# Seven-product up chunks in the first plain feed-forward stage, and the weight sums of the gated stages on VectorE

## What is computed

```python
def _sq_relu_mlp(h, w_up, w_down):            # first block, twice: w_up 1024 x 4096
    u = jax.nn.relu(h @ w_up)
    return (u * u) @ w_down
...
x = x + _sq_relu_mlp(_rmsnorm(x, norm_ffn[i]), mlp_w_up[i], mlp_w_down[i])
...
# second block, four times: gate and up weights side by side, 1024 x (2 * 2816)
x = x + 0.5 * rms_norm(swiglu(rms_norm(x, g[0]), ffn_wgu[i, 0], ffn_wd[i, 0]), g[1])
```

## Time and profile before

| | |
|---|---|
| median of 3 runs | 3510.94 us (3510.49 to 3515.82) |
| the profiled execution | 3511.05 us |
| its span, first to last instruction | 3509.1 us |
| TensorE busy | 3423.1 us |
| VectorE busy | 2336.1 us |
| ScalarE busy | 1423.5 us |
| GpSimd busy | 940.0 us |
| mean granted TensorE clock | 0.991 of full |

### The profile page before, as it was taken

How to read it: one execution, slowest core, us unless ns; L and a number is a source line. 1 busy time by engine, 2 the same in 40 slices (tenths; PEclk the granted TensorE clock), 3 DMA queues, 4 the chain that set the end, 5 groups by cost and what they waited for, 6 DMA issues and landing times. The chain is left out here.

```text
span 3509.1 us, 54575 instructions
## 1 busy us (share of the span) xinstructions
PE 3423.1 (98%) x21451; PEld 2854.4 (81%) x21451; DVE 2336.1 (67%) x3142; ACT 1423.5 (41%) x2011; POOL 940.0 (27%) x627
## 2 busy tenths in 40 slices
PE   8999999999999999999999999999999999999998
PEld 6888888644789979997777789987998787778997
DVE  6665554366677778876567587878777534468786
ACT  5632223365444444334544343344334422244333
POOL 1220002010223325444014145424443000015452
PEclk9999999999999999999999999999999999999999
DMA  3332224100323223232200123222332222213322
GB/s 122 96 112 96 96 96 108 37 1 1 96 96 108 96 84 109 96 108 92 73 26 4 61 96 109 96 95 87 107 107 96 84 84 84 81 52 108 109 97 71
DMA packets 232575, 296.21 MB, mean 84 GB/s; under 512 B 21893, under 2 KB 201464, under 8 KB 232392
## 3 DMA queue, kind: packets, MB, share of 16 engines
q1 hardware_dynamic: 230864, 290.48, 25.6%
q0 software_dynamic: 1152, 3.05, 0.4%
q10 hardware_dynamic: 376, 0.12, 0.0%
HBM read 291.53 MB, written 2.10 MB: 84 GB/s over the span
## 5 line engine op out<-in xcount | busy, mean ns | idle before, releaser
L336 DVE TENSOR_TENSOR wlo<-raw,whi 128x2048 fp32r<-128x2048 f32 x266 | 654.0, 2458 | 265.2 <-ACT whi L330 252.8
L330 ACT ACTIVATE whi<-raw 128x2048 fp32r<-128x2048 f32 x191 | 365.6, 1914 | 691.6 <-PE bank L342 598.8
L340 PE MATMUL bank<-h_hi,whi 128*128 128x512 f32 (+1 forms) x1548 | 616.5, 398 | 23.6 <-DVE h_lo L1135 11.2
L341 PE MATMUL bank<-h_lo,whi 128*128 128x512 f32 (+1 forms) x1548 | 602.7, 389 | 0.0
L342 PE MATMUL bank<-h_hi,wlo 128*128 128x512 f32 (+1 forms) x1548 | 602.6, 389 | 0.0
L340 PE MATMUL bank<-u_hi,whi 128*128 128x512 f32 x1440 | 563.2, 391 | 10.9 <-DVE fsum L850 4.8
L342 PE MATMUL bank<-u_hi,wlo 128*128 128x512 f32 x1440 | 560.7, 389 | 0.0
L341 PE MATMUL bank<-u_lo,whi 128*128 128x512 f32 x1440 | 560.3, 389 | 0.0
L340 PEld LDWEIGHTS bank<-h_hi,whi 128*128 128x128 f32 x1548 | 292.1, 189 | 102.3 <-issue 27.2
L342 PEld LDWEIGHTS bank<-h_hi,wlo 128*128 128x128 f32 x1548 | 292.1, 189 | 61.0
L341 PEld LDWEIGHTS bank<-h_lo,whi 128*128 128x128 f32 x1548 | 292.3, 189 | 60.7 <-issue 3.6
(11 more groups left out here) (487 smaller groups left out, 5959.6 us busy)
## 6 DMA issues: line engine op xcount, KB each, us to landing
raw<-in_ffn_wgu SPq DMA_DIRECT2D x88, 1024.0 KB, 5.1
raw<-in_ffn_wd SPq DMA_DIRECT2D x44, 1024.0 KB, 4.8
raw<-in_mlp_w_up SPq DMA_DIRECT2D x32, 1024.0 KB, 5.3
raw<-in_mlp_w_down SPq DMA_DIRECT2D x32, 1024.0 KB, 4.8
raw<-in_odd_w_in SPq DMA_DIRECT2D x24, 1024.0 KB, 5.1
raw<-in_even_w_in SPq DMA_DIRECT2D x13, 1024.0 KB, 5.3
raw<-in_rg_w_in SPq DMA_DIRECT2D x8, 1024.0 KB, 5.6
raw<-in_odd_w_out SPq DMA_DIRECT2D x8, 1024.0 KB, 5.0
```

Source lines behind the costliest of these rows:

```text
L330: e.activation(whi[:, n % 2, :], raw[:, n % 2, :], ACT.Copy).then_inc(hi_ready, 1)
L336: e.tensor_tensor(wlo[:, n % 2, :], raw[:, n % 2, :], whi[:, n % 2, :].bitcast(F32), ALU.subtract).then_inc(lo_ready, 1)
L340: pe.matmul(o, w_hi, r_hi, start=first, stop=False)
L341: pe.matmul(o, w_hi, r_lo, start=False, stop=False)
```

## The change

f0 gets seven-product up chunks from group 4 on, and f1 from group 4 instead of 5. Both use the same token steps (two tiles before group 2, two before group 3), and both, as the gated stages do already, make the low halves of group 1 only behind the sixth eviction of the first down chunk. GpSimd's token sums wait for all eight token operations instead of four. The sparse mixer's constants, which lie where f0's token tiles now are, are made behind f0's last up chunk, except for the first clearing and the two transfers into `fsum`. The tables for even and odd are made behind the wait for VectorE's sums of the norm instead of ahead of it.

In the gated stages `dve_weights_sums` on VectorE takes the place of `pool_weights`. For the gate chunk of the next group it stands behind the fourth part of the up chunk (in the last plain group: at the end of the group); for the up chunk it stands at the very start of the group. The low copy of the up chunk moves from there to between the third and the fourth part of the gate chunk.

```diff
--- before.py
+++ after.py
@@ -121,7 +121,7 @@
         n_hi_a, n_lo_a = sem("n_hi_a"), sem("n_lo_a")
         w_hi, w_lo = sem("w_hi"), sem("w_lo")
         LEFT, RIGHT = slice(0, S // 2), slice(S // 2, S)
-        w_sum = sem("w_sum")
+        w_sum, v_sum = sem("w_sum"), sem("v_sum")
         xhi_ready, xlo_ready = sem("xhi_ready"), sem("xlo_ready")
         t_scaled, t_sum, t_hi, t_lo = sem("t_scaled"), sem("t_sum"), sem("t_hi"), sem("t_lo")
         seven_act, seven_dve = sem("seven_act"), sem("seven_dve")
@@ -192,7 +192,7 @@
             down = a["ffn_wd_2"][l, i].rearrange("(c k p) n -> c p k n", k=2, p=P)
             return dict(gu=2, groups=NG2, w=[g, u], down=down, swiglu=True, dst=fsum)
 
-        SEVEN = {"f1": 5, "s00": 3, "s01": 3, "s10": 3, "s11": 3}
+        SEVEN = {"f0": 4, "f1": 4, "s00": 3, "s01": 3, "s10": 3, "s11": 3}
 
         def seven(name, g):
 
@@ -456,11 +456,32 @@
             e.wait_ge(w_sum, at(4 * y + 3, i, 4 * k))
             e.tensor_tensor(d[:, XS4], quarter(n, 1, 0), d[:, XS2], ALU.subtract).then_inc(w_sum, 1)
 
+        def gated_no(name, g, c):
+            return seven_no(name, g, c) - seven_no("s00", SEVEN["s00"], 0)
+
+        def dve_weights_sums(e, name, g, c, n, i, dn):
+            y, z = seven_no(name, g, c), 4 * gated_no(name, g, c)
+            d = wsum[(y - seven_base[name]) % 2]
+            e.wait_ge(loaded[n % 2], at(landed[n], i, dn * 8))
+            if (y - seven_base[name]) % 2:
+                e.wait_ge(tiles_out, before[chunk_gu(name, SEVEN[name]) - 1])
+            e.wait_ge(xlo_ready, at(y - 1, i, 4))
+            e.tensor_tensor(d[:, XS3], quarter(n, 0, 0), quarter(n, 0, 1), ALU.subtract).then_inc(v_sum, 1)
+            e.wait_ge(v_sum, at(z + 1, i, 16))
+            e.tensor_tensor(quarter(n, 0, 1), quarter(n, 0, 1), quarter(n, 1, 1), ALU.add).then_inc(v_sum, 1)
+            e.wait_ge(v_sum, at(z + 2, i, 16))
+            e.tensor_tensor(d[:, XS2], quarter(n, 0, 1), quarter(n, 0, 0), ALU.subtract).then_inc(v_sum, 1)
+            e.wait_ge(v_sum, at(z + 3, i, 16))
+            e.tensor_tensor(d[:, XS4], quarter(n, 1, 0), d[:, XS2], ALU.subtract).then_inc(v_sum, 1)
+
         def act_weights(e, name, g, c, n, i, dn, dt, middle=None):
             k = 2 * FFN[name]["gu"]
             y = seven_no(name, g, c)
             e.wait_ge(tiles_out, at(before[n - 1], i, dt))
-            e.wait_ge(w_sum, at(4 * y + 4, i, 4 * k))
+            if FFN[name]["swiglu"]:
+                e.wait_ge(v_sum, at(4 * gated_no(name, g, c) + 4, i, 16))
+            else:
+                e.wait_ge(w_sum, at(4 * y + 4, i, 4 * k))
             e.activation(whi[:, n % 2, :], raw[:, n % 2, :], ACT.Copy).then_inc(hi_ready, 1)
             if middle:
                 middle()
@@ -527,7 +548,7 @@
             for h in range(2):
                 v = [th_raw[:, 2 * h:2 * h + 2, t, 0, :] for t in range(7)]
                 b12 = th_raw[:, 2 * h:2 * h + 2, TB11, 1, :]
-                e.wait_ge(t_scaled, 2 * z + h + 1)
+                e.wait_ge(t_scaled, 2 * z + 2)
                 e.tensor_tensor(v[T1], b12, v[TB11], ALU.subtract).then_inc(t_sum, 1)
                 e.tensor_tensor(v[T3], v[TB22], b12, ALU.subtract).then_inc(t_sum, 1)
                 e.wait_ge(t_sum, 8 * z + 4 * h + 1)
@@ -535,7 +556,7 @@
                 e.wait_ge(t_sum, 8 * z + 4 * h + 3)
                 e.tensor_tensor(v[T4], v[TB21], v[T2], ALU.subtract).then_inc(t_sum, 1)
 
-        TOKEN_STEPS = {"f1": {2: (0,), 3: (1, 2), 4: (3,)}}
+        TOKEN_STEPS = {name: {2: (0, 1), 3: (2, 3)} for name in ("f0", "f1")}
 
         def act_tokens(e, name, ks):
             z = t_no[name]
@@ -701,8 +722,8 @@
 
             def gu(g, n, i, dn, dt):
                 if seven(name, g):
-                    for c in range(f["gu"]):
-                        pool_weights(e, name, g, c, n + c, i, dn)
+                    if not f["swiglu"]:
+                        pool_weights(e, name, g, 0, n, i, dn)
                     return
                 if f["swiglu"]:
                     for j in range(2):
@@ -740,10 +761,11 @@
                         e.wait_ge(uhi_done, at(2 * (b + g - 1) + 2, i, 4))
                     src = part(c, P_E)
                     step(3 * c + 1)
-                    third = tmp[:, 7, LEFT] if meanwhile else d
+                    third = tmp[:, 7, LEFT] if c else d
                     e.tensor_tensor(third, src, snap[:, c, :], ALU.add).then_inc(seven_dve, 1)
                     if meanwhile:
                         meanwhile()
+                    if c and meanwhile:
                         e.wait_ge(ulo_done, at(2 * (b + g - 1) + 2, i, 4))
                     src = part(c, P_C)
                     step(3 * c + 2)
@@ -752,11 +774,14 @@
                 def outer(c, p, d, signal):
                     e.tensor_tensor(d, part(c, p), snap[:, c, :], ALU.add).then_inc(signal, 1)
                 if f["swiglu"]:
+                    dve_weights_sums(e, name, g, 1, n + 1, i, dn)
                     if deferred(name, g - 1):
                         products(g - 1, i)
+                joined(0)
+
+                def low():
                     dve_lo(e, n + 1, i, dn, dt)
-                joined(0)
-                last_quarter(0)
+                last_quarter(0, low if f["swiglu"] else None)
                 if f["swiglu"]:
                     dve_weights_rest(e, name, g, 1, n + 1, i)
                 elif deferred(name, g - 1):
@@ -770,6 +795,8 @@
                 dve_lo(e, n + 2, i, dn, dt)
                 joined(1)
                 last_quarter(1, (lambda: u_low(g - 1, i, (1,))) if deferred(name, g - 1) else None)
+                if seven(name, g + 1):
+                    dve_weights_sums(e, name, g + 1, 0, n + 3, i, dn)
                 src = part(1, P_A2)
                 e.wait_ge(seven_act, at(a0 + 2, i, 2 * acts))
                 e.tensor_tensor(tmp[:, 2, LEFT], src, tmp[:, 0, LEFT], ALU.mult)
@@ -823,8 +850,10 @@
                             e.wait_ge(ulo_done, at(2 * (b + g - 1) + j + 1, i, 4))
                         e.tensor_tensor(tmp[:, 2 + j, :], pbank[half + 2 + j][:, :], tmp[:, j, :], ALU.mult)\
                             .then_inc(prod_done, 1)
-                if not (g == 1 and f["swiglu"] and name in SEVEN):
+                if not (g == 1 and name in SEVEN):
                     u_low(g, i)
+                if f["swiglu"] and seven(name, g + 1):
+                    dve_weights_sums(e, name, g + 1, 0, n + 3, i, dn)
                 if g == 0 and not f["swiglu"]:
                     dve_lo(e, n + f["gu"] + 1, i, dn, dt)
                 if g == 0 and name in SEVEN:
@@ -855,7 +884,7 @@
                         e.tensor_tensor(dst[:, m, :], dst[:, m, :], src[:, :], ALU.add).then_inc(added, 1)
                     if final and early_lo(stage) and m >= 2:
                         lo_tile(e, stage + 1, m - 2)
-                    if m == 5 and g == 0 and f["swiglu"] and name in SEVEN:
+                    if m == 5 and g == 0 and name in SEVEN:
                         u_low(1, i)
                     if final and not early_lo(stage) and m == 1:
                         dve_lo(e, n + 1)
@@ -1032,11 +1061,11 @@
             j = norm_no[stage]
             if PLAN[stage][1] is not None:
                 pool_owed(e, stage)
+                e.wait_ge(n_add, 7 * j + 7)
                 if PLAN[stage + 1] == ("even",):
                     pool_even_early(e, chain)
                 elif PLAN[stage + 1] == ("odd",):
                     pool_odd_early(e, chain)
-                e.wait_ge(n_add, 7 * j + 7)
                 return
             if PLAN[stage - 1][0] == "setup":
                 for k in range(1, 4):
@@ -1737,14 +1766,20 @@
         def slope_of(h):
             return 2.0 ** (-8.0 * (h + 1) / HEADS)
 
+        def pool_nsa_first(e, chain):
+            chain(e.memset(fsum[:, :, :], 0.0))
+            for h in range(2):
+                r = slice(h * HD, h * HD + HD)
+                e.dma_start(w1bd[0][r, :, r], NSA_SMALL[0][0][0].rearrange("(l d) e -> d l e", d=HD)).then_inc(small_in, 16)
+
         def pool_nsa_early(e, chain):
-            chain(e.memset(fsum[:, :, :], 0.0))
+            last = FFN["f0"]["groups"] - 1
+            e.wait_ge(tiles_out, before[chunk_gu("f0", last) + 1])
+            e.wait_ge(gate_done, 2 * (ffn_base["f0"] + last) + 2)
             chain(e.memset(w2bd[:, :, :], 0.0))
             for z, (w1, w2, pe_) in enumerate(NSA_SMALL):
                 for h in range(2):
                     r = slice(h * HD, h * HD + HD)
-                    if z == 0:
-                        e.dma_start(w1bd[z][r, :, r], w1[0].rearrange("(l d) e -> d l e", d=HD)).then_inc(small_in, 16)
                     e.dma_start(w2bd[r, z, r], w2[0]).then_inc(small_in, 16)
                     e.dma_start(perow[0:CMP_LEN, z, r], pe_[0]).then_inc(small_in, 16)
             e.dma_start(gw[:, :, :], cols(nsa_in, D + 6 * 256, 48)).then_inc(small_in, 16)
@@ -3575,11 +3610,12 @@
```

(7 more changed lines are left out.)

## The result

The changed kernel takes 3531.48 us (median of 5 runs, 3529.13 to 3533.4) against 3511.58 for the one before (5 runs, 3510.49 to 3515.82): a ratio of 1.0055, 95% interval 1.004 to 1.007, so 19.9 us slower. The profiled execution took 3529.13 us with a span of 3527.4, which is 18.3 more than the 3509.1 of before. Two runs in a far slower state of the chip, one of the kernel before (4843 us) and one of e11 (6378 us), are left out of all ranges and ratios.

A forecast was written before the change was run, and what follows sets the result against it. TensorE, busy 98% of the span, was the bound. Terms -11.4 - 0.95 - 1.8 - 5.8 - 1.8 + 41.9 = +20.2 on 3511.05 gave 3531, put at 3530.5 us; range 3503 to 3550, its own 3520 to 3545.

The forecast's parts named there:

- f0 and f1, groups: Seven-product groups in f0 from group 4 save 11.4 us; f1 starting at group 4 instead of 5 saves 0.95.
- constants behind the last up chunk: Sparse mixer's constants moved behind f0's last up chunk: at most 19 us within a 21.8 us window, so zero cost.
- First down chunks: First down chunks lose their lateness: 1.8 us gained in f1, 5.8 over four gated stages, nothing lost in f0.
- Norms: Tables made after the norm's sums gain 1.5 us before even and 0.3 before odd; bounds 0 and 3 in all.
- The gated term: Gated stages: sums on VectorE delay TensorE's fifth and seventh products through a chain of order, costing 41.9 us.
- groups 4 to 9: Gated loop groups in four stages: 0.94 us of waits per group, 22.6 us in all.
- group 10: Unrolled gated group: slower sums and a join raise the wait to 1.35 us, 5.4 over four stages.
- Group 3: First seven-product gated pair: late sums make it near 22.7 us; with 0.6 lost ahead each time, 13.9 more.
- rival 1: Gated sums are hidden because VectorE is ahead at the down chunk's end: 3489 us, chance 0.16.
- Rival 2: Waits shorten TensorE's matmul pitch from 0.118 to some 0.113 us, giving back 13.8 us: 3517, chance 0.13.
- Rival 3: VectorE becomes the bound, each gated period longer by another 0.8 to 1.2 us: 3560, chance 0.08.
- Rival 4: Token and norm gains fail, GpSimd's scalings disturbing as before: +6, 3537 us; chance 0.63 together with the forecast.

The follow-up runs named there:

- e11: Version with both moves (e5), TensorE also waiting before each group's second product for the end of its own first product: 3512.08 us, ratio 1.0008.
- e9: Version with both moves (e5), group 1's low halves again ahead of the first down chunk's evictions in f0 and f1: 3495.94 us, ratio 0.9964.
- e6: Changed kernel with GpSimd's token sums again waiting for four token operations instead of eight: 3536.61 us, ratio 1.0076.
- e10: Version with both moves (e5), GpSimd's tables for even and odd again ahead of the wait for the norm's sums: 3494.56 us, ratio 0.9959.
- e5: Changed kernel, ScalarE's first-product copy ahead of its wait for the up chunk's sums, VectorE's low copy behind the fourth part: 3491.08 us, ratio 0.9947.
- e8: Changed kernel plus one useless 256-column VectorE addition per gated group, behind the gate chunk's sums: 3532.94 us, ratio 1.0064.
- run 118: Not a follow-up run: part of the sentence saying that matmuls of 256 columns run 118 ns apart; no kernel or measured time belongs to it.
- e3: Changed kernel with only ScalarE's copy of the gate chunk's first product moved ahead of its wait for the up chunk's sums: 3495.17 us, ratio 0.9959.
- e1: Changed kernel with gated sums back on GpSimd and the up chunk's low copy back ahead of the first join: 3492.75 us, ratio 0.9956.
- e2: Kernel before, with only the gated stages' sums moved to VectorE and the low copy's new place: 3557.83 us, ratio 1.013.

## Why the prediction was right

It gave 3530.5 us, 19.6 above before, with 3531.48 measured. Its steps, each against the changed kernel's trace:

- **f0 and f1, groups.** -11.4 and -0.95 predicted. From the sums of the norm ahead of f0 to those of the norm behind it took 360.0 us and takes 348.7, so -11.3; the same for f1, its first down chunk included, went down by 2.8, with -2.75 predicted. Groups at 20.81 as said; constants behind the last up chunk cost nothing that shows.
- **First down chunks.** f1 -1.8 and gated -5.8 predicted, -1.8 and -6.1 measured: f1 went from 12.64 to 10.88, and the gated stages from 12.33, 12.28, 12.66 and 12.31 to 10.88 each (the one that was read for the prediction stood for all). e9 and e6 give each back by its edit alone. f0 doesn't pay, as said. The reason given for the gated stages, half the operations still disturbed and a lead of 2 us left over, was too careful: two of these operations, which the changed kernel makes last, take 0.74, and evictions start (1296.98) 3.9 us behind the chunk, 1.5 ahead of need.
- **Norms.** -1.5 and -0.3 predicted, -1.45 and -0.23 measured, and 1.5 and 0.3 in e10.
- **The gated term.** +41.9 predicted. The pairs add up to 675.1 against 633.6, 41.5 more, and the four down chunks ahead of group 3 to 1.7 more: +43.2. The chain was named link by link: first sum 0.90 behind the start instead of 0.81, last one done at 3.76 (3.59), copy of the first product at 5.98 (5.81), fourth part at 9.52 (9.26). Two of its terms were a little small. The chained sums are 0.72 us apart, not 0.70, and the extra of a late release falls due at both waits, not once: 0.37 + 0.11 at the fifth product, 0.61 + 0.11 at the seventh, 1.19 per pair against 0.94. Against that stands the shorter pitch: six of the 32 pairs came out 0.41 to 0.43 us shorter than their like (five at 20.55 to 20.65, one of group 3 at 22.02), since behind the seventh product's wait their matmuls ran 0.113 apart. Group 3 was put at 22.7 and is 22.4, the wait ahead of it at 0.6 and is 0.43. So the parts were off by more than their sum: groups 4 to 9 cost 26.8 and not 22.6, group 10 4.9 and not 5.4, group 3 with the wait ahead of it 11.6 and not 13.9. That these errors nearly cancel is luck.
- **What the sum left out.** The steps as measured add up to +21.3 (-11.3 - 2.8 - 6.1 - 1.7 + 43.2), the span to +18.3. The missing 3.0: the start until f0 is 1.3 shorter, the stretch from s00 to s01 is 2.0 shorter beyond its norm's gain, of which 0.75 is a norm at half clock in the kernel before alone, and the sparse mixer is 0.3 longer. The mixer of even itself ran 10.2 us at half clock before and 6.8 after. Among the kept executions of the changed kernel and its variants, which share this code, the start spreads over 2.1 us, the stretch from s00 to s01 over 3.2 and the sparse mixer over more (last section). So a hit within 1 us is luck too; what the prediction can claim is the sign, the mechanism and the size of the main term.
- **Slips of the working.** Group 3's pairs and the waits ahead of them give 11.4 + 4 x 0.6 = 13.8, not 13.9; group 10's parts add up to 1.32, not 1.35; and with a third of the waits left rival 1 comes to 3503, not 3500. None moves the forecast.
- **The rivals.** Rival 1, sums hidden, said 3489 and falls as put: the chain does bind. But its number is e5's, 3491.08: the cover it asked for is there, and only the order keeps the kernel from it. Rival 2, the shorter pitch, was seen in 6 of 32 pairs; e11 shows that a wait by itself doesn't cause it. Rival 3, VectorE at its limit, falls by e8, by sums 0.72 us apart where it asked for 1.0, and by a period of 31.89 where it asked for over 32.3. Rival 4, disturbances that stay, falls by e6 and e10.
- **The rule.** By the Trainium skill (GPSIMD Engine Reference, section 4.1), VectorE is the place for such sums. The trace agrees for the single operation (0.69 against 1.29 us). For the kernel the rule gave no answer: 43 us lost with the sums in this order, none in the loop with e5's.

## What to carry to other kernels

A move of work to a faster engine is priced by what stands behind it in that engine's order, not by its load: here 5.6 us per group fitted under TensorE and still cost it 1.2, since two short operations that TensorE waited for stood behind long copies nobody needed yet. So when an input becomes late, first look at each engine's queue for a short urgent operation behind the one that waits, and move it ahead. A gain and a loss that hide each other, like the 17 and 37 us here, are found by undoing each part alone.

## What the runs showed of the hardware

**Two pitches.** Matmuls of 256 columns run 118 ns apart nearly always, and 113, half of the 227 of 512 columns, behind some waits. e3 mostly alternates between the two from one gated pair to the next (19.41 and 19.90 us from start to start). Its stretches, with ends rounded to 0.1:

```profile
1492.20:1511.70 19.50, 19.50 (x170) 19.43 (x168) 16.87 (x24) 8.00 (x10) 0.00 (x0) 1.00 0.31 102
1552.90:1572.80 19.90, 19.90 (x169) 19.83 (x168) 15.55 (x22) 7.99 (x10) 0.00 (x0) 1.00 0.33 107
```

and the start of the seventh product in the first of them (the first row starts on time, the second 0.22 behind it):

```profile
1500.71 0.38 PE L529 MATMUL bank<-th,x_hi 128*128 128x256 f32 x1
1500.93 0.28 PE L530 MATMUL bank<-th,x_hi 128*128 128x256 f32 x1
1501.04 0.28 PE L531 MATMUL bank<-th,x_lo 128*128 128x256 f32 x1
```

The shorter pitch is worth up to 0.4 us per pair, and lasts until the down chunk (once, in the changed kernel, only until the next wait). What brings it on stays open: the hole in e11 did not, nor did most of the waits of the changed kernel.

**The clock at the norms.** TensorE's granted clock was at half (1.2 GHz) for 3.4 us in four norms of e5 (here two of them, the first with the 3.4 us ahead of it, in which TensorE was busy for 1.71), and at full (2.4 GHz) in e1 in the same place. The stretches of e5:

```profile
1988.50:1991.90 3.40, 1.71 (x12) 1.37 (x12) 3.40 (x8) 1.80 (x5) 0.00 (x0) 1.00 0.00 0
1991.90:1995.30 3.40, 3.40 (x12) 2.72 (x11) 3.14 (x5) 2.50 (x5) 0.00 (x0) 0.50 0.02 5
2346.90:2350.30 3.40, 3.40 (x11) 2.73 (x10) 3.14 (x5) 2.50 (x5) 0.00 (x0) 0.50 0.00 0
```

and of e1:

```profile
1991.90:1995.30 3.40, 2.88 (x13) 2.03 (x12) 3.27 (x6) 2.17 (x4) 0.00 (x0) 1.00 0.02 5
```

Three of them cost some 0.77 us each (102nd matmul at 26.97 instead of 26.20). The fourth lies in the norm's matmuls with ones ahead of s11, which take 6.28 us from first to last instead of 4.59, and costs 1.7. Together that is 4 us. e5's span is 3.9 longer than e1's (3491.2 against 3487.3) though its group 3 costs 1 us less. What brings these stretches on was not tried. So two kernels that differ only in a gated loop can be 4 us apart for a reason far from it.

**The same code, 8 us apart.** No edit touches TensorE's work in the sparse mixer between f0 and f1, and the thirteen profiled executions took from 220.3 to 228.6 us for it. Here are the shortest (e6) and the longest (e2); the third figure from the end is TensorE's mean granted clock:

```profile
631.35:851.68 220.33, 202.59 (x1159) 108.77 (x1157) 133.67 (x464) 131.51 (x372) 19.75 (x12) 0.97 0.05 10
```

```profile
641.22:869.84 228.62, 211.29 (x1158) 113.33 (x1157) 133.91 (x464) 131.85 (x372) 19.77 (x12) 0.93 0.05 10
```

The clock was at half for 13.7 us of it in e6 and for 34.1 in e2. In between it goes roughly the same way: 222.9 to 223.8 us with 20 to 24 at half, 223.2 to 226.0 with 27. So a stage that an edit leaves alone has to be taken out before two spans are compared, and a single profile doesn't measure an effect of a few us by its span.

**A late release costs more than its lateness**, by 0.10 to 0.11 us, since the second matmul follows at 0.22 instead of 0.118.
